# Eight modulation products spread over four column groups of the matmul array

## The reference

```
mod_x = jax.nn.silu(c) @ ada_w[l] + ada_b[l]
sh1, sc1, g1, sh2, sc2, g2 = jnp.split(mod_x[:, None, :], 6, axis=-1)
mod_c = jax.nn.silu(c_ctx) @ ada_w[l] + ada_b[l]
csh1, csc1, cg1, csh2, csc2, cg2 = jnp.split(mod_c, 6, axis=-1)
hc = modulate(rmsnorm(ctx, norm1_g[l]), csh1, csc1)
pc = hc @ w_in[l]
...
hx = modulate(rmsnorm(x, norm1_g[l]), sh1, sc1)
px = hx @ w_in[l]
```

## Time and profile before

| | us |
|---|---|
| timed runs | 2299.1, 2306.67, 2311.11 |
| span of the profiled execution | 2299.4 |
| PE busy | 2214.0 (96%) |
| DVE, ACT, POOL busy | 895.4, 830.7, 882.8 |
| first product with `w_in` starts at | 66.93 |
| second one (f0) starts at | 79.69 |

### The profile page before, as it was taken

The page is one execution under the profiler, slowest core; times in us unless marked ns, Lnnn a source line. Parts: engine busy times, 40 slices in busy tenths (PEclk is TensorE's granted clock), DMA queues, the critical chain, the costliest instruction groups (busy, mean ns, idle before and its releaser), DMA issues.

```text
span 2299.4 us, 28706 instructions
## 1 busy us (share of the span) xinstructions
PE 2214.0 (96%) x11528; PEld 1834.8 (80%) x11528; DVE 895.4 (39%) x1411; ACT 830.7 (36%) x1208; POOL 882.8 (38%) x640
## 2 busy tenths in 40 slices
PE   6999999999999989999999999999999999999998
PEld 3777778878888868979797878788888988888886
DVE  2457855441211246564747420505143344222102
ACT  3355433232322335242424323535323443222212
POOL 0335943434444434030321244132254625444442
PEclk9999999999999999989999999999999999999999
DMA  6412333422233233020301122131332412222321
GB/s 235 147 55 68 116 103 112 163 73 92 92 102 99 92 108 101 20 74 6 105 20 55 37 92 92 38 110 38 110 110 92 147 56 91 92 91 97 104 91 55
DMA packets 179968, 205.89 MB, mean 90 GB/s; under 512 B 3364, under 2 KB 170768, under 8 KB 179472
## 3 DMA queue, kind: packets, MB, share of 16 engines
q1 hardware_dynamic: 176912, 195.17, 26.2%
q10 hardware_dynamic: 2944, 9.15, 1.1%
HBM read 198.01 MB, written 6.29 MB: 89 GB/s over the span
## 4 chain that ended last, share of the span: by engine, by line
PE 83%; DVE 6%; ACT 2%; POOL 2%; issue 1%; DMA 1%; DVEq 0%; ACTq 0%; SPq 0%
PE ps L2071 20%; PE ps L2073 20%; PE ps L2072 20%; PE ps L2180 4%; PE ps L2587 2%; PE ps L2392 2%; PE ps L2600 2%; POOL w_lo L688 2%; PE ps L2671 2%; PE ps L2688 1%; PE ps L2358 1%; PE ps L2118 1%; PE ps L2120 1%; PE ps L2119 1%; ACT w_hi L760 1%
## 5 line engine op out<-in xcount | busy, mean ns | idle before, releaser
L688 POOL TENSOR_TENSOR w_lo<-raw,w_hi 128x512 fp32r<-128x512 f32 x586 | 780.6, 1364 | 1353.0 <-ACT w_hi L760 1353.0
L2071 PE MATMUL ps<-h_hi,w_hi 128*128 128x512 f32 x1384 | 560.4, 405 | 12.9 <-DVE h_lo L1407 4.8
L2073 PE MATMUL ps<-h_hi,w_lo 128*128 128x512 f32 x1384 | 545.3, 394 | 0.0
L2072 PE MATMUL ps<-h_lo,w_hi 128*128 128x512 f32 x1384 | 544.2, 393 | 0.0
L760 ACT ACTIVATE w_hi<-raw 128x2048 fp32r<-128x2048 f32 x150 | 285.7, 1905 | 371.0 <-PE ps L2073 363.6
L2071 PEld LDWEIGHTS ps<-h_hi,w_hi 128*128 128x128 f32 x1384 | 263.0, 190 | 74.3 <-issue 10.5
L2073 PEld LDWEIGHTS ps<-h_hi,w_lo 128*128 128x128 f32 x1384 | 262.8, 190 | 56.9
L2072 PEld LDWEIGHTS ps<-h_lo,w_hi 128*128 128x128 f32 x1384 | 263.2, 190 | 52.4 <-issue 1.2
L2071 PE MATMUL ps<-g_hi,w_hi 128*128 128x512 f32 x256 | 101.0, 394 | 0.0
L2073 PE MATMUL ps<-g_hi,w_lo 128*128 128x512 f32 x256 | 100.4, 392 | 0.0
L2072 PE MATMUL ps<-g_lo,w_hi 128*128 128x512 f32 x256 | 99.4, 388 | 0.0
(11 more groups left out here) (417 smaller groups left out, 3856.4 us busy)
## 6 DMA issues: line engine op xcount, KB each, us to landing
raw<-w_in SPq DMA_DIRECT2D x48, 1024.0 KB, 5.2
raw<-w_down SPq DMA_DIRECT2D x27, 1024.0 KB, 5.1
raw<-ada_w SPq DMA_DIRECT2D x24, 1024.0 KB, 5.2
raw<-w_gate_up SPq DMA_DIRECT2D x22, 1024.0 KB, 5.0
raw<-w_up SPq DMA_DIRECT2D x16, 1024.0 KB, 5.4
raw<-w_mkv SPq DMA_DIRECT2D x8, 1024.0 KB, 5.4
raw<-w_out SPq DMA_DIRECT2D x4, 1024.0 KB, 5.5
xT<-bias_band SPq DMA_DIRECT2D x2, 2048.0 KB, 9.9
```

The lines of the kernel that those rows point to most:

```text
L688: ins = nc.gpsimd.tensor_tensor(w_lo[:, split_at[u] % 2, cols], raw[:, u % 2, cols], w_hi[:, split_at[u] % 2, cols].bitcast(F32), ALU.subt ...
L2071: T.matmul(out_, wh, hi, start=start, stop=False, skip_group_check=True)
L2072: T.matmul(out_, wh, lo, start=False, stop=False, skip_group_check=True)
L2073: return T.matmul(out_, wl, hi, start=False, stop=stop, skip_group_check=True)
```

## The change

The weights of the eight ada products become 32 columns wide (`silu_wide`), with the two vectors in columns 0 and 1 and zeros in the other 30. The eight matmuls of a unit go in turn to four column groups: slices 0 and 4 write PSUM rows 0 to 31, slices 1 and 5 rows 32 to 63, and so on. Each group adds up two slices. ACT copies all 128 rows in place of two. The matmul that turns the rows now contracts over 128 rows with a table `pick` that has a one where row mod 32 is 0 or 1, which adds the four partial sums. DVE clears `silu_wide` once, ACT makes two more small activations, the constants table grows from 512 to 514 columns, and the first ada product waits for four activations where it waited for two.

```diff
-for _name, _cols in [("ident", P), ("ones", P), ("tri", P), ("incl", P)]:
+for _name, _cols in [("ident", P), ("ones", P), ("tri", P), ("incl", P), ("pick", 2)]:
...
+            "incl": i[:, None] >= i[None, :], "pick": i[:, None] % 32 == np.arange(2)[None, :]}
...
-    ada_row = r("ada_row", [2, 2, 256])
+    ada_row = r("ada_row", [P, 2, 256])
+    silu_wide = r("silu_wide", [P, KT, 32])
...
+            act.wait_ge(sem["wide_zeroed"], 1)
+            for i, name in enumerate(("c", "c_ctx")):
+                nc.scalar.activation(silu_wide[:, :, i], vecT[:, VEC_AT[name]:VEC_AT[name] + KT], ACT.Silu).then_inc(sem["c_silu"], 1)
...
-                nc.scalar.activation(ada_row[:, a % 2, :], ps[0:2, a % 2, 0:256], ACT.Copy).then_inc(sem["ada_rowed"], 1)
+                nc.scalar.activation(ada_row[:, a % 2, :], ps[:, a % 2, 0:256], ACT.Copy).then_inc(sem["ada_rowed"], 1)
...
+            V.memset(silu_wide[:, :, :], 0.0).then_inc(sem["wide_zeroed"], 1)
...
-                    pe.wait_ge(sem["c_silu"], 2)
+                    pe.wait_ge(sem["c_silu"], 4)
...
-                    ins = T.matmul(ps[0:2, a % 2, 0:256], silu_c[:, k, :], raw[:, u % 2, k * 256:(k + 1) * 256],
-                                   start=k == 0, stop=k == KT - 1)
+                    rows = slice(32 * (k % 4), 32 * (k % 4 + 1))
+                    ins = T.matmul(ps[rows, a % 2, 0:256], silu_wide[:, k, :], raw[:, u % 2, k * 256:(k + 1) * 256],
+                                   start=k < 4, stop=k >= 4, skip_group_check=True)
...
-                                   const[0:2, CONST_AT["ident"]:CONST_AT["ident"] + 2], start=True, stop=True)
+                                   const[:, CONST_AT["pick"]:CONST_AT["pick"] + 2], start=True, stop=True)
```

More of the change, by code:

```diff
@@ L68, in shape_constants @@
     cols = {"ident": np.eye(P), "ones": np.ones((P, P)), "tri": i[:, None] <= i[None, :],
-            "incl": i[:, None] >= i[None, :]}
+            "incl": i[:, None] >= i[None, :], "pick": i[:, None] % 32 == np.arange(2)[None, :]}
     const = np.concatenate([np.asarray(cols[n], np.float32) for n in CONST_AT], axis=1)
@@ L432, in build @@
     ada_mod lat_gained lat_inv qk_mm qk_normed scl2_done at_scores at_prob at_out_lo fc_mm fc_half fc_split fz_done fm_lo_done
-    y_lo_done g_lo_done ab_turned gate_cum c_normed kv_turned k_scaled qd_done kk_mm nL_done inv0_done lv_mm
+    y_lo_done g_lo_done ab_turned wide_zeroed gate_cum c_normed kv_turned k_scaled qd_done kk_mm nL_done inv0_done lv_mm
     lv_done r_o r_ws r_u r_st o_scaled o_turned oa_lo_done rb_done gate_silu gate_scaled s_lo_done""".split()
```

## The result

The changed kernel takes 2307.44 us (median of 20 runs, 2303.22 to 2316.88) where the kernel before takes 2302.3 us in the same runs. The ratio is 1.0023, with a 95% interval of 1.0013 to 1.0034: 3.0 to 7.8 us slower. The forecast was 3 us faster. The profiled span is 2301.4 us, 2.0 more than before.

A forecast was written before the change was run, and what follows sets the result against it. TensorE bounds the kernel (PE 83% of the chain), so its dense work must start earlier: three units at 1.5 us make 4.5, cut to 3 for the clock; 2306.7 - 3 = 2303.7, stated as 2303.5 us, range 2293 to 2312.

The forecast's parts named there:

- The price of a unit: Each ada unit on TensorE: 2.1 us in place of 3.62, 1.5 us less, with half the records overlapping.
- my lower bound of 1.03: Each ada unit if all four column groups run at once: 1.03 us, 2.6 less.
- rival 2: Ada units: all four groups at once, 2.6 us off each, about -6 in all, 2300.7 us; chance 0.13.
- rival 3: Ada units: bare weight loads add 1.6 us each, 4.8 on three units, 2311.5 us; chance 0.12.
- The clock: Before ada_mm(6): longer idling may bring 1.2 GHz, that unit 4.0 us not 2.1; gain 1.7 to 4.5, taken as 3.
- What reaches the path: Start up to f0: three units' worth, 3 x 1.5 = 4.5 us at full clock; ada_mm(0) and ada_mm(2) gains lost.
- The larger constants table is loaded ahead of `x`: 1 KB more, nothing: Constants table load at the start: 1 KB more to load ahead of `x`, costing nothing.
- From f0 on ... the shift stays: After the f0 product starts: no wait is tied to an absolute time, so the lead lasts to the end.
- My own sign of being wrong: At f0: wrong if it starts later than 79.7, or starts as said and the span does not follow.
- The rivals: Ada units: no overlap (chance 0.25), all four groups at once (0.13), bare weight loads (0.12), against half overlap (0.5).
- The bound of 0.5%: Whole kernel time: about 0.5%, 11.5 us, is what can be told from no change; no case reaches it alone.

The follow-up runs named there:

- experiment 6: experiment 1 plus 31 products of constants by constants, output unread, where TensorE waits: 2292.87 us against 2299.49 for the kernel before, ratio 0.9979.
- experiment 2: Kernel before with 32 unused bytes behind the constants table, no other change: 2314.66 us against 2299.89, ratio 1.0051.
- experiment 1: The change with one_eps put in the constants table's unused end, so sq2, acc, tmp2 and all regions keep old addresses: 2297.69 us against 2299.89, ratio 0.9987.
- experiment 9: The change with 224 more bytes behind the constants table, later buffers 256 bytes beyond the kernel before: 2298.51 us against 2300.93, ratio 0.9990.
- experiment 3: Kernel before with 64 unused bytes behind the constants table: 2308.76 us against 2299.89, ratio 1.0034.
- experiment 4: Kernel before with only s_hi and s_lo (and gate, gu behind them) moved by 32 bytes: 2301.56 us against 2299.89, ratio 1.0003.
- experiment 7: Kernel before with y moved by 96 bytes (first block only), g by 128, s by 512, om by 256: 2309.13 us against 2299.49, ratio 1.0029.
- experiment 8: Kernel before with 256 unused bytes behind the constants table: 2301.58 us against 2300.93, ratio 1.0011.

## Why the prediction was wrong, step by step

- **The price of a unit: mis-sized.** I took 2.1 us, on the ground that both halves of a slice keep their group busy. It is 1.07 at full clock, my lower bound of 1.03: rival 2. In the first unit four records run at once, and eight start within 0.26 us (0.64 us to the last one's end):

```profile
17.89 0.42 PE L2197 MATMUL ps<-raw,silu_wide 128*32 128x256 f32 x4 [1.58 <-DMA raw<-ada_w]
```

```profile
17.89 0.64 PE L2197 MATMUL ps<-raw,silu_wide 128*32 128x256 f32 x8 [1.58 <-DMA raw<-ada_w]
```

  The next four start 0.22 us after the first four, the time of the array for one record. The trace doesn't say which half of a slice a record is. That the two halves follow one another in their group, with the other three groups beside them, fits the rows and is not shown. What I had wrong is the order of starts, which let only two records overlap. The weight loads (106 to 178 ns) did not show as time: rival 3 is excluded.
- **The clock: the direction right, the extent too small.** I allowed for one slow unit. All units but the first and part of the third ran at 1.2 GHz. TensorE, done sooner, idled longer in the gaps, and experiment 6, which fills them, has most units at the full clock. 1.94 us at the low clock is close to my 2.1 at the full one, so the sum came out near by two errors against each other: that is luck.
- **What reaches the path: the chain right, its terms not.** Forecast for the f0 start 75.2 to 78, best estimate 3 us earlier; measured 77.06, 2.6 earlier, still behind POOL. But I had ada_mm(3) start 1.5 us earlier than before, at 35.5, and it started at 37.31, 0.3 later: the turns of `ctx` took 3.50 us at the low clock in place of 2.18, and `acc` came only 0.8 us earlier. So the lat_q load went out at 39.30 (forecast 37.6) and the seventh unit began at 56.89 (55.2), each 1.7 late. That unit then took 1.93 us where I had 4.0 for the low clock, and this gave it back. That ada_mm(0) and ada_mm(2) gain nothing was right: the next thing waited 3.75 us for its load and 2.04 us for DVE.

```profile
34.65 1.02 PE L2170 MATMUL ps<-const,acc 128*128 128x1 f32 x4 [2.04 <-DVE acc L1387]
```

- **"The larger constants table is loaded ahead of `x`: 1 KB more, nothing": this step failed.** I costed the transfer and did not ask what the two columns do to the addresses behind them. They moved every later buffer by 32 bytes. The price is 10.9 us by the rows of experiment 2 and 8 to 15 by its time; between the change (1.0023) and experiment 1 (0.9987) it is about 8 us. The gain is 2.6 to 4 us. With them went the step **"From f0 on ... the shift stays"**: the paces that were untouched in experiments 1 and 9 bear it out. My own sign of being wrong was met: f0 started as said and the span did not follow.
- **The rivals.** None of mine was this mechanism. The slower one named bare weight loads, at 2311.5 us; the time came out on its side for another reason. That 2307.44 us lies in my range of 2293 to 2312 says nothing for the forecast: the range was made wide by the spread of single runs, around a median of three runs (2306.7) that is 4.4 us above that of twenty (2302.3).
- **The bound of 0.5%: right as a size, wrong as a limit.** All versions lie within it except experiment 2 at 1.0051. But I took it for what can be told from no change, and with twenty runs a side the interval is 0.1% to either side, so that the 0.23% is clear.

## What to carry to other kernels

When a change adds a column to a table or a field to a buffer, ask which buffers lie behind it: TensorE's pace on a moving operand changed by 2% with its place here, and no waiting time showed it. Compare the time from the first to the last start of an untouched operand's matmuls in both traces; where it differs, pad the addition (here to 256 bytes) before judging the change itself. And where a faster product only lengthens TensorE's gaps, the clock may take back about half, as here (4.2 us of a lead of 7 to 8): look at the granted clock of the stretch, not only at the gap, and in more than one profile.

## What was not expected of the hardware

- The pace of an fp32r matmul stream of 512 columns depended on where its moving operand lies: 687 ns for three at the old address and 256 or 512 bytes further, 701 at 32, 698 at 64 (`s`), 16 ns more at 96 (`y`) and 13 ns more at 128 (`g`). `h` in another place has its own values: 6 ns more for three when moved by 4928 bytes. Why is open. Weights are loaded while the matmuls run (97.66 us of the 119.00), but no run separates this from other causes.
- fp32 matmuls of 32 output rows in four column groups ran four records at a time: at the full clock a unit's 3.62 us became 1.07.
- The same start, run again, met the low clock at other times: 3.4 us of it before 69 us in the profile of the kernel before, 7 to 14 us in those of experiments 2, 3, 4, 7 and 8.
